# Softmax weights turned in 32x32 blocks on VectorE and moved by SBUF transfers, in a two-layer transformer kernel

## What is computed

```python
def dsa_attention(q, k, v, q_idx, k_idx, w_idx):      # layer one: top 64 keys by an index score
    ...
        p = jax.nn.softmax(s, axis=-1).astype(v.dtype)
        return jnp.einsum('bhtj,btjhd->bthd', p, v_sel)

def moba_attention(q, k, v):                          # layer two, first branch
    ...
        p = jax.nn.softmax(jnp.concatenate([s_sel, s_own], axis=-1), axis=-1).astype(v.dtype)
        ...
def mla_attention(q_nope, q_rope, k_nope, k_rope, v): # layer two, second branch
    ...
        s = jnp.where((kpos[None, :] <= qpos[:, None])[None, None], s, -jnp.inf)
        p = jax.nn.softmax(s, axis=-1).astype(v.dtype)
        return jnp.einsum('bhqk,bkhd->bqhd', p, v)
```

## Time and profile before

| what | value |
|---|---|
| median of 3 runs | 2383.08 us (2382.54 to 2383.17) |
| the profiled execution, its own time | 2383.49 us |
| its span in the trace | 2381.6 us |
| TensorE busy | 2365.1 us, 99% |
| VectorE, ScalarE, GpSimd busy | 58%, 50%, 5% |
| TensorE clock granted, mean | 0.998 of full |

### The profile page before, as it was taken

One profiled execution on the slowest core, in us unless ns is written; L12 is line 12 of the kernel. 1 busy time (PEld: TensorE's weight loads), 2 busy tenths in 40 slices (PEclk: granted clock), 3 DMA queues, 4 the chain that ended last, 5 costly groups with the idle time before them and its releaser, 6 DMA issues.

```text
span 2381.6 us, 29812 instructions
## 1 busy us (share of the span) xinstructions
PE 2365.1 (99%) x10624; PEld 1958.6 (82%) x10624; DVE 1390.7 (58%) x1574; ACT 1194.4 (50%) x1489; POOL 128.8 (5%) x228
## 2 busy tenths in 40 slices
PE   9999999999999999999999999999999999999997
PEld 7788888888888888888888888888888888888886
DVE  6785465776766765555554554766555555555543
ACT  6455455666666544445455544555444444444442
POOL 0100010000000000002130000122000000000000
PEclk9999999999999999999999999999999999999999
DMA  8775467788787766666776556666777777776554
GB/s 303 194 206 173 146 224 211 217 225 216 205 226 219 207 215 202 203 203 195 202 193 198 162 164 186 210 219 215 211 201 200 210 202 210 202 200 221 194 194 136
DMA packets 443082, 483.52 MB, mean 203 GB/s; under 512 B 208000, under 2 KB 225808, under 8 KB 442864
## 3 DMA queue, kind: packets, MB, share of 16 engines
q1 hardware_dynamic: 437712, 474.83, 67.7%
q0 software_dynamic: 4704, 6.44, 1.0%
q10 hardware_dynamic: 576, 1.05, 0.1%
HBM read 448.12 MB, written 2.10 MB: 189 GB/s over the span
## 4 chain that ended last, share of the span: by engine, by line
PE 97%; SPq 1%; issue 0%; DMA 0%; ACT 0%; DVE 0%; POOLq 0%; POOL 0%; DVEq 0%; ACTq 0%
PE acc L727 31%; PE acc L729 31%; PE acc L728 31%; SPq L504 1%; PE pair_banks L898 1%; PE bank L718 0%; PE pair_banks L929 0%; PE acc L753 0%; PE acc L757 0%; PE acc L760 0%; DMA w_raw<-in_w_in 0%; PE pair_banks L959 0%; PE pair_banks L870 0%; PE pair_banks L930 0%; SPq L373 0%
## 5 line engine op out<-in xcount | busy, mean ns | idle before, releaser
L1430 DVE TENSOR_TENSOR w_lo<-w_raw,w_hi 128x1024 fp32r<-128x1024 f32 (+1 forms) x842 | 1024.7, 1220 | 928.3 <-ACT w_hi L1068 926.7
L1068 ACT ACTIVATE w_hi<-w_raw 128x1024 fp32r<-128x1024 f32 (+1 forms) x842 | 886.2, 1055 | 1051.4 <-PE acc L729 1003.3
L727 PE MATMUL acc<-w_hi,xT 128*128 128x512 f32 (+1 forms) x2208 | 862.7, 391 | 0.0
L729 PE MATMUL acc<-w_hi,xT 128*128 128x512 f32 (+1 forms) x2208 | 857.1, 388 | 0.0
L728 PE MATMUL acc<-w_lo,xT 128*128 128x512 f32 (+1 forms) x2208 | 856.6, 388 | 0.0
L727 PEld LDWEIGHTS acc<-w_hi,xT 128*128 128x128 f32 x2208 | 414.6, 188 | 86.9 <-issue 2.3
L729 PEld LDWEIGHTS acc<-w_hi,xT 128*128 128x128 f32 x2208 | 414.5, 188 | 85.7
L728 PEld LDWEIGHTS acc<-w_lo,xT 128*128 128x128 f32 x2208 | 414.7, 188 | 83.5
L727 PE MATMUL acc<-w_hi,f_hi 128*128 128x512 f32 x688 | 267.6, 389 | 0.0
L728 PE MATMUL acc<-w_lo,f_hi 128*128 128x512 f32 x688 | 267.6, 389 | 0.0
L729 PE MATMUL acc<-w_hi,f_lo 128*128 128x512 f32 x688 | 267.6, 389 | 0.0
(11 more groups left out here) (220 smaller groups left out, 1308.4 us busy)
## 6 DMA issues: line engine op xcount, KB each, us to landing
w_raw<-in_w_up SPq DMA_DIRECT2D x264, 512.0 KB, 4.2
w_raw<-in_w_in SPq DMA_DIRECT2D x198, 512.0 KB, 3.8
w_raw<-in_w_down SPq DMA_DIRECT2D x176, 512.0 KB, 4.6
w_raw<-in_w_gate SPq DMA_DIRECT2D x88, 512.0 KB, 3.6
w_raw<-in_w_out SPq DMA_DIRECT2D x64, 512.0 KB, 4.6
w_raw<-in_w_branch_a SPq DMA_DIRECT2D x16, 512.0 KB, 4.2
w_raw<-in_w_branch_b SPq DMA_DIRECT2D x16, 512.0 KB, 4.8
halves<-stage SPq DMA_DIRECT2D x208, 32.0 KB, 2.6
```

Source lines behind the costliest of these rows:

```text
L727: pe.matmul(o, l, w_hi[:, slot, k, 0:width], start=start, stop=False)
L729: last = pe.matmul(o, m, w_hi[:, slot, k, 0:width], start=False, stop=stop)
L1068: act.activation(in_slot(w_hi, slot, width), in_slot(w_raw, slot, width), ACT.Copy).then_inc(w_split_hi, 1)
L1430: dve.tensor_tensor(in_slot(w_lo, slot, width), in_slot(w_raw, slot, width), in_slot(w_hi, slot, width).bitcast(F32), ALU.subtract).then_i ...
```

## The change

The six turns on TensorE and the two copies on ScalarE of each attention pair go. `norm` is followed on VectorE by one transposition of 32x32 blocks of all 768 columns, from `pbuf` to a spare buffer (`p_source`). SyncE moves the blocks to `pT` in 16 transfers, four behind each of four loads (`move_p`, steps a+3 to a+6). `pv` moves from step a+6 to a+9 and to PSUM bank 0, and waits for all 16 transfers; `split_y` moves to a+10. GpSimd issues no transfer any more: for pieces 0 to 2 of x and of the mix SyncE issues all 16 transfers, four in each of the steps b to b+3, and `split_x` and `split_mix` stand in b+7 instead of b+3; for piece 3 SyncE issues 8 and ScalarE the other 8 in step b, and the split stays in b+3. The constants and `pool_w` are loaded by SyncE. Three moves of layer two's queries start 2 or 4 steps later, and `copy_k` of `ka` 2 steps later.

```diff
+        later = {("qn", 1): 2, ("qr", 2): 4, ("qa", 1): 4}.get((name, half), 0)
         for b in range(4):
-            put(n + lead + b, "move", u, g, b)
+            put(n + lead + later + b, "move", u, g, b)
         if name in ("k1", "ka"):
-            put(n + lead + 6, "copy_k", u, g)
+            put(n + lead + (6 if name == "k1" else 8), "copy_k", u, g)
...
-        put(a + 3, "norm", which)
-        put(a + 4, "turn_p", which)
-        put(a + 5, "copy_p", which)
-        put(a + 6, "pv", which, pair)
-        put(a + 7, "split_y", which, pair)
+        put(a + 3, "norm", which, pair)
+        for b in range(4):
+            put(a + 3 + b, "move_p", which, pair, b)
+        put(a + 9, "pv", which, pair)
+        put(a + 10, "split_y", which, pair)
...
-            put(b, "move_x", 0)
-            put(b, "move_x", 1)
-            put(b + 3, "split_x", n, gain)
+            for part in range(4) if n < 3 else (None,):
+                put(b + (part or 0), "move_x", n + 4 * quarters, part)
+            put(b + (7 if n < 3 else 3), "split_x", n, gain)
...
-        put(b, "move_mix", 0); put(b, "move_mix", 1); put(b + 3, "split_mix", n)
+        for part in range(4) if n < 3 else (None,):
+            put(b + (part or 0), "move_mix", n, part)
+        put(b + (7 if n < 3 else 3), "split_mix", n)
...
+        def move_blocks_of(queue, part, first_half, to, from_, done):
+            for k in range(4) if part is not None else range(8):
+                b, a_ = (part, k) if part is not None else (k // 2, k % 2 + (0 if first_half else 2))
+                move_block(queue, to, from_, b, a_).then_inc(done, 16)
+        def move_x(queue, n, part, first_half):
+            queue.wait_ge(x_blocks, NT * (n + 1))
+            move_blocks_of(queue, part, first_half, flat_stage[1], flat_stage[0], x_moved)
...
+            def move_p(which, pair, b):
+                if b == 0:
+                    p_count[0] += 1
+                    sp.wait_ge(p_blocks, p_count[0])
+                from_ = p_source(which, pair).rearrange("p (n b k) -> p n b k", b=4, k=32)
+                for a_ in range(4):
+                    to = pT[32 * b:32 * (b + 1)].rearrange("p (n a k) -> p n a k", a=4, k=32)[:, :, a_]
+                    sp.dma_start(to, from_[32 * a_:32 * (a_ + 1), :, b]).then_inc(p_moved, 16)
...
             def on_pv(which, pair):
-                wait_bank(2)
-                pe.wait_ge(copy_done, pvs[0])
+                wait_bank(0)
+                pvs[0] += 1
+                pe.wait_ge(p_moved, 256 * pvs[0])
...
+            def on_move_x(n, part):
+                if part is None:
+                    move_x(act, n, part, False)
+            def on_move_mix(n, part):
+                if part is None:
+                    move_mix(act, n, part, False)
...
-                    last = dve.tensor_tensor(v, v, pinv[:, 2 * blk:2 * blk + 2].unsqueeze(2).to_broadcast([P, 2, nk]), ALU.mult)
-                last.then_inc(p_ready, 1)
+                    link(dve.tensor_tensor(v, v, pinv[:, 2 * blk:2 * blk + 2].unsqueeze(2).to_broadcast([P, 2, nk]), ALU.mult))
+                linked()
+                dve.transpose(p_source(which, pair), pbuf).then_inc(p_blocks, 1)
```

More of the change, by code:

```diff
@@ L373, in move_block, with move_mix, p_source @@
             return queue.dma_start(dst, src)
-        def move_x(queue, count, half):
-            count[half] += 1
-            queue.wait_ge(x_blocks, NT * count[half])
-            for b in range(4):
-                for a_ in range(2 * half, 2 * half + 2):
-                    move_block(queue, flat_stage[1], flat_stage[0], b, a_).then_inc(x_moved[half], 16)
-        def move_mix(queue, count, half):
-            count[half] += 1
-            queue.wait_ge(mix_blocks, count[half])
-            for b in range(4):
-                for a_ in range(2 * half, 2 * half + 2):
-                    move_block(queue, flat_half, flat_stage[1], b, a_).then_inc(mix_moved[half], 16)
+        def move_blocks_of(queue, part, first_half, to, from_, done):
[5 more added lines that the diff above has]
+            move_blocks_of(queue, part, first_half, flat_stage[1], flat_stage[0], x_moved)
+        def move_mix(queue, n, part, first_half):
+            queue.wait_ge(mix_blocks, n + 1)
+            move_blocks_of(queue, part, first_half, flat_half, flat_stage[1], mix_moved)
+        def p_source(which, pair):
+            if which == "one":
+                v = over_y[7 if pair < 3 else 5][:]
+            else:
+                v = flat_stage[0] if which == "moba" and pair >= 2 else over_y[5][:]
+            return v[:, 0:2 * KEYS]
         def turned(unit, q):
@@ L453, in _ @@
         def _(sp):
-            chunk, products, x_moves, mix_moves = Count(), Count(), [0, 0], [0, 0]
+            chunk, products, p_count = Count(), Count(), [0]
             def load_x(n):
@@ L908, in on_scores @@
                 free[2] = free[3] = (scores_masked, atts.now)
-            def on_turn_p(which):
-                wait_bank(0, 1)
-                pe.wait_ge(p_ready, atts.now)
-                for j in range(2):
-                    turn(0, j * S, pbuf[:, j * P:(j + 1) * P])
-                    last = turn(0, j * S + P, pbuf[:, S + j * S:S + j * S + P])
-                last.then_inc(copy_full, 1)
-                for j in range(2):
-                    last = turn(1, j * P, pbuf[:, S + j * S + P:S + (j + 1) * S])
-                last.then_inc(copy_full, 1)
-                copies.now += 2
-                free[0], free[1] = (copy_done, copies.now - 1), (copy_done, copies.now)
-                pvs[0] = copies.now
             def on_pv(which, pair):
-                wait_bank(2)
-                pe.wait_ge(copy_done, pvs[0])
+                wait_bank(0)
+                pvs[0] += 1
+                pe.wait_ge(p_moved, 256 * pvs[0])
+                tiles = pT.rearrange("p (n s) -> p n s", n=6)
                 for j in range(2):
                     v = operands(which, pair, j)[2]
-                    pe.matmul(T[2][:, j * S:(j + 1) * S], v[:, 0], pT[:, j * S:(j + 1) * S], start=True, stop=False)
-                    last = pe.matmul(T[2][:, j * S + P:(j + 1) * S], v[:, 1], pT[:, 2 * S + j * P:2 * S + (j + 1) * P],
-                                     start=False, stop=True)
+                    pe.matmul(T[0][:, j * S:(j + 1) * S].rearrange("p (n s) -> p n s", n=2), v[:, 0],
+                              tiles[:, j:3 + 2 * j:2 + j], start=True, stop=False)
+                    last = pe.matmul(T[0][:, j * S + P:(j + 1) * S], v[:, 1], tiles[:, 3 + 2 * j], start=False, stop=True)
                 last.then_inc(split_full, 1)
                 splits.now += 1
-                free[2] = (split_lo, splits.now)
+                free[0] = (split_lo, splits.now)
             def on_pool_d(n, g):
@@ L1166, in on_exp @@
                 last.then_inc(exp_done, 1)
-            def on_copy_p(which):
-                copied(pT[:, 0:2 * S], 0)
-                copied(pT[:, 2 * S:3 * S], 1, S)
             def on_copy_d(n):
@@ L1196, in on_split_y @@
                 k = 2 * pair + (0 if which == "moba" else 8)
-                high([y_hi[:, k:k + 2].rearrange("p a b -> p (a b)")], 2)
+                high([y_hi[:, k:k + 2].rearrange("p a b -> p (a b)")], 0)
+            def on_move_x(n, part):
[4 more added lines that the diff above has]
+                    move_mix(act, n, part, False)
             def on_split_x(n, gain):
                 n_x[0] += 1
-                for half in range(2):
-                    act.wait_ge(x_moved[half], 16 * 8 * n_x[0])
+                act.wait_ge(x_moved, 256 * n_x[0])
                 for q in range(4):
@@ L1218, in on_split_mix @@
             def on_split_mix(n):
-                for half in range(2):
-                    act.wait_ge(mix_moved[half], 16 * 8 * (n + 1))
+                act.wait_ge(mix_moved, 256 * (n + 1))
                 for q in range(4):
@@ L1523, in on_mask, with on_norm @@
                 last.then_inc(scores_masked, 1)
-            def on_norm(which):
+            def on_norm(which, pair):
                 dve.wait_ge(exp_done, n_att[0])
```

75 lines of the change are left out of this document (38 added, 37 removed).

## The result

| | before | after |
|---|---|---|
| median | 2383.08 us (2382.54 to 2383.52, 5 runs) | 2395.75 us (2391.16 to 2396.93, 5 runs) |
| ratio | | 1.0050, 95% interval 1.0038 to 1.0063 |
| span of the profiled execution | 2381.6 us | 2395.1 us |
| from the last eviction of TensorE's results to the end of the span | 12.8 us | 7.5 us |

The change made the kernel slower by 12.7 us. The forecast was 5.2 us slower, 2388.3, with a range up to 2394.0: the direction was right, the time lies 1.75 us above the range. The sum left out one kind of loss and one kind of gain altogether, so the miss is larger in its parts than in its total.

A forecast was written before the change was run, and what follows sets the result against it. TensorE, busy 99% of the span, was taken as the bound. Terms: +4.6 + 4.1 + 0.9 + 5.7 - 10.1 = +5.2 us, giving a median forecast of 2388.3 us, range for 8 in 10 2380 to 2394.

The forecast's parts named there:

- (1): Attention pairs: removing the six turns on TensorE saves 0.67 us a pair, 8.0 us over 12 pairs.
- (2): Layer two: three TensorE waits go, of 0.84 (key copy), 0.57 and 0.68 us, together 2.1 us gained.
- (3): Piece 2's later split: TensorE waits 1.6 us at two feed-forward joints and 1.4 at the mix, sum 4.6 us.
- (4): Joints and mix: ScalarE's eight issues, 0.64 us each, delay the weight chunk queued behind them; 4.1 us lost in all.
- (5): Products with v wait for SyncE's moves: 5.7 us at the first two `moba` pairs, 0.9 for the other ten together.
- (6): VectorE's block transposition, constants and `pool_w` on SyncE, and loads delayed by moves: all cost nothing.
- cheap issue: Block moves cost ScalarE and SyncE 0.45 us or less, so most waits go: 2380 to 2383 us; chance 0.20.
- full cover: TensorE never waits for (3) to (5), so only the gain is left: 2373 us; chance 0.05.
- dear turns: Each turn takes its whole 0.27 us from the stream, so 11.7 us more are gained: 2377 us; chance 0.04.
- Every product with v waits: Landings of 3.6 us and more make ten pairs wait 0.5 to 1 us more, `moba` too: 2393 to 2400; chance 0.16.
- the last rival: Weight ring runs dry: SyncE falls 12 us behind in steps 421 to 443, giving 2396 us or more; chance 0.05.

The follow-up runs named there:

- e9: As e8, but GpSimd issues eight of each pair's sixteen weight moves at once and SyncE the other eight in two steps; 2367.43 us, ratio 0.9936 to the kernel before.
- e5: Changed kernel with each mix piece's 16 moves issued at once, 8 by SyncE and 8 by GpSimd, split still seven chunks behind; 2388.02 us.
- e1: Changed kernel with the split of pieces 0 to 2 six chunks behind the piece instead of seven; 2397.60 us.
- e10: Kernel before with the softmax part alone: block transposition on VectorE, sixteen moves a pair on SyncE, products with v three chunks later; 2402.12 us.
- e7: Changed kernel with the sixteen moves of each pair's weights issued by GpSimd instead of SyncE; 2392.37 us.
- e8: Changed kernel with GpSimd issuing weight moves, piece 3's second half and half the mix moves (at once), split at six chunks; 2373.52 us, ratio 0.9962 to the kernel before.

## Why the prediction was wrong, step by step

(1), (2) *Turns and waits that go: right.* By TensorE's own products, six pairs took 4.4 us less, 0.74 a pair, where 0.67 stood (the 4.9 of the table holds 0.5 us of a late eviction); in e9, where nothing hides it, the four pairs of layer one are worth 2.7, just under 0.7 each. The key copy's 0.84 us is there: the lag of TensorE's products against the old trace falls from 9.27 to 8.43 us at its place (1185.55 us in the old trace).

(3) *The split four chunks later: right at the feed-forward joints, mis-sized at the mix.* 1.38 + 0.16 at both, against 1.6. At the mix 5.59 against 1.4. The step assumed ScalarE free of its weight chunk at 0.26 + 1.06 us there too. It waited 3.33 us for the load of that chunk, as four of SyncE's moves now stand before each of three loads, and the first set starts only when VectorE has its blocks. The prediction had used VectorE's late blocks, 5.12 us, in (4) and not for the loads queued behind SyncE's moves. e5 shows it.

(4) *ScalarE's eight issues: right in mechanism and size.* 5.38 to 5.43 us for eight, 0.67 each against 0.64; 1.88 at `w_in_2`, 0.20 and 0.24 at the other joints, against 1.8, 0.2 and 0.2. At the mix nothing, since TensorE was already late. e1 shows that (3) and (4) take each other's place.

(5) *Products with v: the `moba` pairs right in sum, the ten others too low.* 4.18 + 0.75 against 2.9 + 2.8. The first two pairs of layer one waited 0.82 and 2.34, against 0.9 for all ten; the other eight waited nowhere over 0.2. At the first pair the way from the normalising products to the data took 16.3 us, as forecast (16.5), but the normalising started 2.9 us later than in the old trace and TensorE's products there only 0.2 us later, so nothing of the 0.9 us to spare was left. ScalarE's exponentials had waited 2.32 us for VectorE's maxima; why those were late stays open. At the second pair SyncE issued the first move 3.6 us after the blocks were there, behind moves of queries.

(6) *Constants at no cost: mis-sized.* 1.60 us and 1.4 in the stage; partly chance, as the variants show.

*What no step had.* This is where the prediction failed. First the clock: 7.1 us, the largest part of the miss, which came with waits that the prediction itself had at 1.8 and 2.9 us and, in its two parts at the mix, 1.4 and 1.9, and with the one of 2.34 us in layer one that it had near nothing. It priced a wait at its idle time and a restart of 0.16 us; the trace of before, whose longest wait behind the start is 0.68 us, has no row for more. Second the end: -5.4 us, which the trace of before showed in GpSimd's DRAIN, on the line that closes the program. "GpSimd issues no transfers" was costed only in its removal from the stream. Without this gain the result would have been 2401; so the sum was 13.6 us too low in the stream and 5.3 too high behind it. Of the 13.6, 7.1 are the clock, 2.7 the mix's wait beyond its forecast and 2.8 the idle time of the pairs of layer one beyond theirs; 1.0 is spread over the rest.

Of the rivals, cheap issue, full cover and dear turns are refuted (0.67 us an issue, five places with waits, 0.67 us a pair). "Every product with v waits" is too: eight of twelve don't. SyncE's fall behind the ring, which the last rival had at 0.05 in steps 421 to 443, is real there and at the mix, and in e10 it becomes the bound.

## What to carry to other kernels

Price a wait of a dense TensorE stream by its length and by the clock behind it: here 2 us of waiting could cost 3.7, and several waits below 1.6 us can be cheaper than one above 2. When a queue gets more transfers, add up its issues step by step against TensorE's step (here a load and four moves take 3.24 us against 2.72) and ask for each load behind them, also where a move waits for another engine. Read what the engines do on the program's last line too: an engine that issues transfers may be the last to finish there.

## What the runs showed of the hardware

- *TensorE's clock behind waits.* Of all waits over 0.9 us in the thirteen profiles after the start, none of the 27 up to 1.62 us had half clock behind it; of the 15 from 1.78 to 2.34 us six had, and one and the same wait of 1.87 to 1.88 us at `w_in_2` had it in two of six kernels' profiles; all 18 of 2.9 us and more had. One such stretch loses 1.7 us of full clock; behind the waits of 4.7 us and more it is mostly twice that, part of it inside the wait. That a wait of this length has it or not may be why the changed kernel's runs lie 5.8 us apart and those of the one before 1; no run tests it.
- *Issue prices of the same kind of move* (32 partitions, 24 to 32 KB): SyncE 0.64, ScalarE 0.67, GpSimd 0.53 to 0.56 us. GpSimd stood still for 1.2 to 6.6 us within eight of 24 sets of sixteen weight moves (e7, e8), and in none of the twelve sets of eight in e9; but one of e9's sets of eight moves of x had a pause of 1.27 us behind the sixth. The three longest pauses ended 1.22 us after the landing of the last move that it had issued.
- *GpSimd's DRAIN* at the end of the program: 0.65 us without own transfers, 11.1 with 134, but 8.02 with 248: the count alone doesn't set it.
